# Latent attention: one key projection for two heads, another order of rotary product and taps, and a LayerNorm sum placed elsewhere

## The reference, cut to what matters

```python
def conformer_conv(conv_in, conv_w, conv_b, ln_g, ln_b, w_conv_out):
    a, gt = jnp.split(conv_in, 2, axis=-1)
    z = a * jax.nn.sigmoid(gt)
    z = lax.conv_general_dilated(...)          # 31 taps, one filter per channel, 512 channels
    z = layer_norm(z + conv_b, ln_g, ln_b)
    return jax.nn.silu(z) @ w_conv_out

def mla_attention(c_q, c_kv, k_rope_raw, cos, sin, ...):   # 8 heads
    q = rms_norm_2(c_q, q_norm_g) @ w_uq       # 384 -> 8 * (64 + 32)
    kv = rms_norm_2(c_kv, kv_norm_g) @ w_ukv   # 256 -> 8 * (64 + 64)
    q_rope, k_rope = apply_rope(...), apply_rope(k_rope_raw, cos, sin)
    ... # per head: softmax of q_nope @ k_nope + q_rope @ k_rope, causal, times v
    return o @ w_mla_out
```

## Time and profile before

| | |
|---|---|
| median of 3 runs | 2503.52 us (2503.4 to 2503.57) |
| profiled execution | 2503.53 us, of it span 2501.7 us |
| PE busy | 2487.2 us (99%) |
| DVE busy | 1991.2 us (80%) |
| ACT busy | 1244.3 us (50%) |
| POOL busy | 305.2 us (12%) |
| steps 0 to 17 of the latent attention | 1811.5 to 1979.2 us of the span |

### The profile page before, as it was taken

The page is one execution under the profiler, slowest core; times in us unless marked ns, Lnnn a source line. Parts: engine busy times, 40 slices in busy tenths (PEclk is TensorE's granted clock), DMA queues, the critical chain, the costliest instruction groups (busy, mean ns, idle before and its releaser), DMA issues.

```text
span 2501.7 us, 36450 instructions
## 1 busy us (share of the span) xinstructions
PE 2487.2 (99%) x14212; PEld 2186.6 (87%) x14212; DVE 1991.2 (80%) x2830; ACT 1244.3 (50%) x1975; POOL 305.2 (12%) x250
## 2 busy tenths in 40 slices
PE   9999999999999999999999999999999999999998
PEld 7999988889999889999888899998888888888887
DVE  7878867778888688887777888876899786788873
ACT  6444444444444454444554544445577535654552
POOL 4000001320000000000023100000187221200002
PEclk9999999999999999999999999999999999999999
DMA  5333332223333323334323233334333333233331
GB/s 158 99 96 99 101 104 84 80 87 100 99 102 108 112 85 99 102 98 122 101 60 93 80 104 97 112 103 136 86 74 78 126 93 110 84 108 105 102 100 59
DMA packets 487297, 246.83 MB, mean 99 GB/s; under 512 B 42321, under 2 KB 483926, under 8 KB 486870
## 3 DMA queue, kind: packets, MB, share of 16 engines
q1 hardware_dynamic: 486674, 244.19, 33.9%
q10 hardware_dynamic: 452, 0.32, 0.0%
HBM read 240.27 MB, written 4.19 MB: 98 GB/s over the span
## 4 chain that ended last, share of the span: by engine, by line
PE 95%; DVE 2%; ACT 1%; issue 0%; DMA 0%; POOL 0%; DVEq 0%
PE bank L893 8%; PE bank L892 8%; PE bank L891 8%; PE bank L774 6%; PE bank L776 6%; PE bank L775 6%; PE psS L913 4%; PE psS L914 4%; PE psS L915 4%; PE bank L1452 3%; PE psT L957 2%; PE psT L958 2%; PE psT L959 2%; PE psT L774 2%; PE psT L776 2%; PE psT L775 2%
## 5 line engine op out<-in xcount | busy, mean ns | idle before, releaser
L2267 DVE TENSOR_TENSOR wlo<-raw,whi 128x1024 fp32r<-128x1024 f32 (+2 forms) x212 | 289.0, 1365 | 49.2 <-ACT whi L1582 45.9
L774 PE MATMUL bank<-xhl,whi 128*128 128x512 f32 x672 | 264.7, 394 | 0.0
L775 PE MATMUL bank<-xhl,whi 128*128 128x512 f32 x672 | 262.1, 390 | 0.0
L776 PE MATMUL bank<-xhl,wlo 128*128 128x512 f32 x672 | 262.0, 390 | 0.0
L891 PE MATMUL bank<-xshl,whi 128*128 128x256 f32 x840 | 238.0, 283 | 0.0
L893 PE MATMUL bank<-xshl,wlo 128*128 128x256 f32 x840 | 238.0, 283 | 0.0
L892 PE MATMUL bank<-xshl,whi 128*128 128x256 f32 x840 | 237.9, 283 | 0.0
L1582 ACT ACTIVATE whi<-raw 128x1024 fp32r<-128x1024 f32 (+2 forms) x209 | 214.5, 1030 | 37.3 <-PE bank L776 20.4
L2330 DVE TENSOR_TENSOR wlo<-tw,whi 128x1024 fp32r<-128x1024 f32 x140 | 171.6, 1226 | 61.5 <-ACT whi L1622 61.3
L913 PE MATMUL psS<-hhi,whi 128*128 128x512 f32 x488 | 191.8, 393 | 0.0
L914 PE MATMUL psS<-hlo,whi 128*128 128x512 f32 x488 | 191.7, 393 | 0.0
(11 more groups left out here) (703 smaller groups left out, 7099.7 us busy)
## 6 DMA issues: line engine op xcount, KB each, us to landing
raw<-in_ffn_wg SPq DMA_DIRECT2D x88, 512.0 KB
raw<-in_ffn_wu SPq DMA_DIRECT2D x88, 512.0 KB
raw<-in_w_in SPq DMA_DIRECT2D x53, 512.0 KB
raw<-in_w_mlp SPq DMA_DIRECT2D x40, 512.0 KB
raw<-in_ffn_wd SPq DMA_DIRECT2D x48, 256.0 KB
raw<-in_ffn_wd SPq DMA_DIRECT2D x24, 448.0 KB
raw<-in_ffn_wd SPq DMA_DIRECT2D x48, 192.0 KB
raw<-in_ffn_wd SPq DMA_DIRECT2D x48, 128.0 KB
```

The costliest lines, as they stand in the source:

```text
L774: pe.matmul(dest, a, rhs_hi(k), start=start and k == 0, stop=False)
L775: pe.matmul(dest, a, rhs_lo(k), start=False, stop=False)
L776: mm = pe.matmul(dest, b_, rhs_hi(k), start=False, stop=stop and k == tiles - 1)
L2267: dve.tensor_tensor(wlo[:, a:a + n], raw[:, a:a + n], whi[:, a:a + n].bitcast(F32), ALU.subtract).then_inc(s_split, 1)
```

## The change

- Keys: `w_ukv`'s key columns of heads h and h+1 (h even) are loaded together, 128 columns, and projected at once; head h's key comes out in rows 0 to 63 of the bank, head h+1's in rows 64 to 127. Odd heads have no key projection. Their query comes out with the rotary rows first (32 columns and their swapped halves in rows 0 to 63) and the rest in rows 64 to 127, so that it meets its key; the rotary table and the key's rotary rows exist in both places (one more ACT copy).
- The odd head's key stays in `bank[1]` until the step after its partner's projection (steps 3, 7, 11), where ACT and DVE take it out behind the exponentials and the reciprocal; before step 0 for head 1.
- Head units are split only as far as they are filled: 640 columns for even heads, 384 for odd ones, where it was 1024.
- Queues: in steps 4, 8 and 12 DVE makes the rotary product (heads 3, 5, 7) ahead of the taps; in step 8 the eviction, too, is ahead of the taps; in step 0 the split comes after the rotary product. ACT copies the query's other rows ahead of the head's weight split.
- LayerNorm: the two additions of squares stand at the end of DVE's step 13, where they stood in step 14 behind the row maxima; the variance comes behind the reciprocal of step 14; on PE the sum of squares goes in ahead of tile 7 of step 14's unit, where it was tile 5.
- Several semaphores get a second user later in the program and a new name for it (not shown in the diff below).

```diff
+        HEAD_PARTS = [("q", 0), ("k", 0), ("k", 1), ("q", 1)]
+        for h in range(2, H2, 2):
+            HEAD_PARTS += [("q", h), ("k", h), ("k", h + 1), ("q", h + 1)]
+        HEAD_TILES = {C_IN + ORDER.index(("head", h)): QC if h % 2 else QC + KVC for h in range(H2)}
...
+        def head_rows(h):
+            return (slice(NOPE, P), slice(0, NOPE)) if h % 2 else (slice(0, NOPE), slice(NOPE, P))
+
+        ROPE_FIRST = range(4, 2 * H2 - 2, 4)
...
-                    for a, col, n in ((0, i * QK, QK), (QK, r0 + HALF, HALF), (QK + HALF, r0, HALF)):
+                    if i % 2:
+                        parts = ((0, r0, ROPE), (ROPE, r0 + HALF, HALF), (ROPE + HALF, r0, HALF), (NOPE, i * QK, NOPE))
+                    else:
+                        parts = ((0, i * QK, QK), (QK, r0 + HALF, HALF), (QK + HALF, r0, HALF))
+                    for a, col, n in parts:
                         sp.dma_start(dq[:, :, a:a + n], c2(wq, 0, QC, col, n)).then_inc(landed[slot(c)], 16)
-                    sp.dma_start(dk, c2(t["w_ukv_2"], 0, KVC, i * P)).then_inc(landed[slot(c)], 16)
+                    for k in range(0 if i % 2 else KVC):
+                        sp.dma_start(dk[:, k].rearrange("p (h n) -> p h n", h=2), vw[:, k, i:i + 2, 0, :]
+                                     ).then_inc(s_kw if k else landed[slot(c)], 16)
...
-                    elif s // 2 < H2:
-                        pe.wait_ge(h_lo, 2 * (s // 2) + 2)
+                    elif s // 2 < H2 and s // 2 % 2 == 0:
+                        pe.wait_ge(h_lo, head_part("k", s // 2 + 1))
...
-                in_unit(*FILL[s], ready=(lambda k: conv_square_sums() if k == 5 else None) if s == LN_VAR + 1 else None)
+                in_unit(*FILL[s], ready=(lambda k: conv_square_sums() if k == 7 else None) if s == LN_VAR + 1 else None)
...
-                if s % 2 == 0 and h < H2:
+                if s % 2 == 0 and h < H2 and h % 2 == 0:
                     pe.wait_ge(s_i2, evicted(*FILL[s]))
                     project(h, "k")
...
-                a, n = slot(c) * UNIT, tiles * P
+                a, n = slot(c) * UNIT, HEAD_TILES.get(q + c, tiles) * P
...
+            act.activation(rope[0:NOPE, :], rope[NOPE:P, :], ACT.Copy).then_inc(s_rs, 1)
...
+                if s % 4 == 3 and (s + 3) // 2 < H2:
+                    head_k((s + 3) // 2)
...
-                if s == LN_VAR + 1:
-                    for j in (0, 2):
-                        dve.wait_ge(s_lsq, j + 2)
-                        dve.tensor_tensor(ln_sq[j][:, :], ln_sq[j][:, :], ln_sq[j + 1][:, :], ALU.add).then_inc(s_tap, 1)
-                    variance(LNVAR, tap_b, CW, SUMLN)
...
                 if s == LN_VAR + 1:
+                    variance(LNVAR, tap_b, CW, SUMLN)
                     newton(LNVAR, acc)
...
-                if s in (4, 6):
+                if s in (4, 6, 8):
                     evict(*FILL[s])
+                if s in ROPE_FIRST:
+                    head_rope(h)
+                if s % 4 == 3 and (s + 3) // 2 < H2:
+                    head_k((s + 3) // 2)
                 if s:
                     taps(DVE_SHARE.get(("slot", s), 0))
...
-                    if s != 2:
+                    if s > 2 and s not in ROPE_FIRST:
                         head_rope(h)
...
+                if s == LN_VAR:
+                    for j in (0, 2):
+                        dve.wait_ge(s_lsq, j + 2)
+                        dve.tensor_tensor(ln_sq[j][:, :], ln_sq[j][:, :], ln_sq[j + 1][:, :], ALU.add).then_inc(s_tap, 1)
-                if s % 2 == 0 and h < H2:
+                if s % 2 == 0 and h < H2 and h % 2 == 0:
                     head_k(h)
```

More of the change, by code:

```diff
@@ L1130, in project @@
                     mm = pe.matmul(dest, wl, chunk(lath, l0 + k), start=False, stop=k == n - 1)
-                mm.then_inc(h_q if part == "q" else s_used, 1)
+                mm.then_inc(h_q if part == "q" and h % 2 == 0 else s_used, 1)
             def mla_scores(s):
@@ L1907, in glu_tanh, with head_copy, head_scaled @@
                 act.activation(g, g, ACT.Tanh, scale=0.5).then_inc(s_th, 1)
-            def head_q(h):
-                bb = h % 2 * S
-                act.wait_ge(h_q, h + 1)
+            def head_copy(h):
+                rows = head_rows(h)[0]
+                if h % 2:
+                    act.wait_ge(s_used, unit_of("head", h) + 1)
+                else:
+                    act.wait_ge(h_q, h // 2 + 1)
                 if h == 1:
                     act.wait_ge(s_z, 3)
-                act.activation(tmp[0][0:NOPE, :], bank_of[("hq", h)][0:NOPE, :], ACT.Copy).then_inc(h_cp, 1)
+                act.activation(tmp[0][rows, :], bank_of[("hq", h)][rows, :], ACT.Copy).then_inc(h_cp, 1)
+            def head_scaled(h):
+                bb = h % 2 * S
                 act.wait_ge(h_rp, h + 1)
@@ L1919, in head_k @@
             def head_k(h):
-                bb = h % 2 * S
-                act.wait_ge(s_used, unit_of("head", h) + 1)
-                act.activation(k2h[0:NOPE, bb:bb + S], bank_of[("hk", h)][0:NOPE, :], ACT.Copy).then_inc(h_hi, 1)
+                bb, rows = h % 2 * S, head_rows(h)[0]
+                act.wait_ge(s_used, unit_of("head", h - h % 2) + 1)
+                if h >= 2:
+                    act.wait_ge(a_sc, ATT1 + 2 * h - 2)
+                act.activation(k2h[rows, bb:bb + S], bank_of[("hk", h - h % 2)][rows, :], ACT.Copy).then_inc(h_hi, 1)
             split(unit_of("q", 2) + AHEAD, 0)
@@ L1973, in _ @@
                 some = min(share, 1)
+                left = share
                 split(unit_of(*FILL[s]) + AHEAD, 0)
-                if s:
+                if s > 1:
                     products(some)
+                    left -= some
                 if s < MLA_STEPS:
@@ L2023, in _ @@
                     act.activation(pt2h[:, :], psT[:, 0:(TB + 1) * P], ACT.Copy).then_inc(a_th, 1)
-                products(share - (3 * some if s else 1))
-                if s % 2 == 0 and h < H2:
+                products(left)
+                if s % 2 == 0 and h < H2 and h % 2 == 0:
                     head_k(h)
@@ L2059, in cross_qhi @@
             def cross_qhi(h):
-                act.wait_ge(s_x2, h + 1)
-                act.activation(chunk(q3h, h), tmp[h % 2][:, :], ACT.Copy).then_inc(s_x2h, 1)
+                act.wait_ge(s_qs, 5 * L + h + 1)
+                act.activation(chunk(q3h, h), tmp[h % 2][:, :], ACT.Copy).then_inc(s_qh, 1)
             def cross_khi(h):
@@ L2726, in head_rope @@
             def head_rope(h):
-                dve.wait_ge(h_q, h + 1)
+                rows = head_rows(h)[1]
+                if h % 2:
+                    dve.wait_ge(s_used, unit_of("head", h) + 1)
+                else:
+                    dve.wait_ge(h_q, h // 2 + 1)
                 if h == 1:
                     dve.wait_ge(s_z, 3)
-                dve.tensor_tensor(tmp[0][NOPE:P, :], bank_of[("hq", h)][NOPE:P, :], rope[NOPE:P, :], ALU.mult).then_inc(h_rp, 1)
+                    dve.wait_ge(s_rs, 4)
+                dve.tensor_tensor(tmp[0][rows, :], bank_of[("hq", h)][rows, :], rope[rows, :], ALU.mult).then_inc(h_rp, 1)
             def head_q(h):
                 bb = h % 2 * S
-                dve.wait_ge(h_hi, 2 * h + 1)
+                dve.wait_ge(h_hi, head_part("q", h))
                 dve.scalar_tensor_tensor(q2l[:, bb:bb + S], tmp[0][:, :], QK ** -0.5,
@@ L2791, in _ @@
             for j in range(2):
-                for n, r in enumerate((NOPE, QK)):
+                for n, r in enumerate(KEY_ROPE_AT[j]):
                     dve.wait_ge(s_krh, 2 * j + n + 1)
@@ L2855, in _ @@
                     glu(2)
+                    head_rope(h)
+                    split(unit_of(*FILL[s]) + AHEAD, 0)
                 if s == 2:
@@ L2868, in _ @@
                     dve.tensor_tensor(tmp[2][:, :], chunk(zc, 0), chunk(zc, 2), ALU.add).then_inc(s_tap, 1)
-                if s not in (0, 2, 4, 6):
+                if s not in (0, 2, 4, 6, 8):
                     evict(*FILL[s])
```

103 lines of the change are left out of this document (55 added, 48 removed).

## The result

The changed kernel takes 2512.01 us (median of 6 runs, 2510.46 to 2512.58) against 2503.44 (6 runs, 2503.30 to 2503.57): a ratio of 1.0033, 95% interval 1.0023 to 1.0043. It is 8.6 us slower; the prediction said 2505.6, in a range up to 2508.8. The profiled execution took 2511.57 us, 8.0 more than the one of before. One execution of run a_two, further down, ran at a mean granted clock of 0.65 and took 3505.64 us; it was the one that was profiled, and it is left out of that run's figures.

A forecast was written before the change was run, and what follows sets the result against it. PE was taken to bound the kernel, with DVE nearly as full in the attention steps. The terms -5.4 + 4.3 + 1.1 + 0.3 + 1.2 + 1.2 - 0.35 - 0.25 = +2.1 on 2503.5 gave 2505.6 us, range 2501.8 to 2508.8.

The forecast's parts named there:

- POOL's hold on DVE: Steps 4 and 8: the moved split and query low part fall beside POOL's tap additions; +1.2 us, bound 3.8.
- rival (c): Step 12: the 4.3 us standstill makes PE's clock fall; 6 us at half speed cost 3.0, giving 2508.6; chance 0.13.
- Key projections, -5.4: Steps 0, 4, 8 and 12: six matmuls each go, 1.36 us a step, -5.4 us on PE.
- Step 12, +4.3: LayerNorm's sum: PE waits for DVE's chunk addition, since head 7's rotary product stands ahead of the taps; +4.3 us.
- the eight transposes: Sign for rival (c): after the start's standstill, transposes took 0.25 us each against 0.14 in step 8, suggesting a slow restart.
- Scores of steps 10 and 6: PE waits there because DVE's work in steps 8 and 4 grows behind the early rotary product; +1.1 and +0.3 us.
- key projection of step 10: DVE comes late to step 10, so PE waits for the eviction that this projection needs; +1.2 us.
- LayerNorm, -0.35: Step 14: the sum of squares, two tiles later, should find its additions ready, removing PE's 0.35 us wait.
- Scores of step 4, -0.25: The 0.27 us wait before these scores should go, since DVE's split of step 2 has fewer columns; -0.25 us.
- At nothing: Shorter splits of steps 6 and 10, low parts moved into steps 3, 7, 11, ACT's table copy, extra DMA issues: no cost.
- (d): Steps 4 and 8: POOL's full bound of 3.8 us instead of 1.2, giving 2508.2; chance 0.07.

The follow-up runs named there:

- a_two: Changed kernel with two taps instead of four between head 7's rotary product and the chunk addition in step 12: 2509.07 us.
- b_k1: Kernel before the change with the key projections of odd heads cut to one matmul of six, nothing else changed: 2503.21 us.
- a_rope12_poolcut: a_rope12 with POOL's additions of taps cut to 32 of 512 columns, the rest left out: 2499.40 us.
- a_rope12: Changed kernel with head 7's rotary product put back behind the taps of step 12; heads 3 and 5 stay ahead: 2505.42 us.
- a_rope12_ln: a_rope12 with the LayerNorm part undone too: additions of squares at the head of step 14, their sum behind the sixth tile: 2508.68 us.
- a_poolcut: Changed kernel with POOL's additions of taps cut to 32 of 512 columns, the rest left out: 2504.79 us.
- a_rope0: Changed kernel with all rotary products of odd heads behind the taps, as before the change: 2504.68 us.
- a_three: Changed kernel with three taps instead of four between head 7's rotary product and the chunk addition in step 12: 2511.77 us.
- v3: Changed kernel with taps moved into DVE's idle time, step 10's eviction ahead of taps, and ACT's key copy ahead of the tap products: 2503.94 us.

## Why the prediction was wrong, point by point

Two steps of the prediction failed. It put POOL's hold on DVE at +1.2 us, with a bound of 3.8, and cutting POOL's additions gives back 6.0. And its sum put the fall of the clock, which it had as rival (c), at nothing, where the trace shows 2.5. That is 4.8 and 2.5 of the 6.4 us between forecast and measurement; the other terms come to -0.9 together. The change is slower, where no difference was forecast.

- **Key projections, -5.4.** PE does lose these matmuls: from the query projection of step 0 to the next scores it is 1820.49 - 1818.45 = 2.04 us, where before 1.36 more came. The size of the term is right, but the removal does not pay "directly". b_k1 keeps 0.3 of 4.5, so alone it is worth nothing that can be told; only with POOL out of the way (a_rope12_poolcut) are 4.1 of the 5.4 kept. The prediction read that DVE was as full as PE, and drew from it some chains, but not that the whole stretch had no room: from the scores of step 1 to those of step 12 DVE stands idle for 2.4 of 104.5 us in the trace of before.
- **Step 12, +4.3.** Right: 3.99 of waiting, 4.2 from where PE could have started, at the instruction and for the reason that were named. a_rope12 shows it; 0.3 of waiting would be there without the swap.
- **Clock, rival (c).** Given 0.13, and it came: 2.5 us by the trace, and by the medians 6.6 less 3.7, 2.9. No row gave the 6 us at half speed that its price was worked out from; it was 5.2. That the gaps of the trace of before were too short to show a fall was true, but it was no reason against one. Its sign for a slow restart, the eight transposes, doesn't hold either: the granted clock reads 1.00 there too (6.00 to 8.00). The Trainium skill (TensorE: Matmul & The Clock Gate, section "Part 1: The HAM clock gate"), which the prediction named, says that the clock falls back after idling. In this case the trace agrees, the clock being 0.50 behind the standstill and 1.00 before it.
- **Scores of steps 10 and 6, +1.1 and +0.3; key projection of step 10, +1.2.** The three waits are there and are 1.2, 1.2 and 1.7 us (1907.40 to 1909.05 less 0.48, 1867.14 to 1868.79 less 0.48, 1918.83 to 1920.97 less 0.46). Without POOL's additions 0.75 at the scores of step 10 and 0.83 at the key projection remain, and this view shows none at the scores of step 6: what the chains alone give, 1.6.
- **POOL, +1.2, bound 3.8.** The term that was mis-sized most: 6.0. The bound took the two instructions which the change moves, in each of steps 4 and 8. In these four the trace of the changed kernel has 3.3 us of stretch (a split of 1.96, low parts of 1.78 and 1.78), so as a bound for them it was good. But 7.4 of the 10.7 lie in other instructions, and most splits of steps 1 to 11 were already stretched in the trace of before (1440 ns in the median, 1215 without POOL). There it cost 0.3; the longer steps of PE covered it, and part of that cover is what the change removes.
- **LayerNorm, -0.35.** The wait is gone, as said, but its worth is larger: in the new order the old place would wait 2.02 (a_rope12_ln). The 0.35 in the trace of before showed that DVE's chain ends there, and not what that place costs once PE comes to it sooner.
- **Scores of step 4, -0.25.** It failed: 0.31 us of waiting there and 0.26 in step 2, since DVE's splits in steps 1 and 2 are no shorter in time.
- **At nothing.** The low part of the probabilities in steps 5 and 9 (1.9) and the unit of step 7 (0.6) were not. Both are gone in a_poolcut, so they are part of POOL's 6.0.
- **Rivals as if they excluded each other.** (c) and (d) came together. From the runs: 6.6 (the order of step 12) + 6.0 (POOL) - 4.1 (what a_rope12_poolcut is under before) = +8.5, and 8.6 was measured. These are differences along one chain of kernels, so that they add up says little; what checks the terms is the last: -5.4 + 1.6 (the chains without POOL) - 0.35 = -4.15, against -4.1. The range ended at 2508.8 because each rival was added to the forecast alone; with the prices of (c) and (d) together it would have ended near 2511.2.

What stays open: why the clock falls in some executions and not in others behind the same waits, and how much of the spread of 2 us between runs of the changed kernel that is; and how POOL's 6.0 divide between the larger stretch, the lost cover and ACT's waits for POOL.

## What to carry to other kernels

Where two engines are full in the same stretch, work taken from one of them may be worth nothing until the other gets shorter too; test it first by leaving the work out in the old kernel, which here would have shown 0.3 us for 4.5. Look for instructions whose longest duration is far above their shortest in the old trace: such a stretch may be free today (0.3 us here) and cost when its cover is removed (6.0). And don't put an instruction that waits for a late result of the bound engine ahead of ready work on which that engine waits next: here one such swap cost 3.7 us of waiting and 2.5 of clock.

## What the runs showed of the hardware that was not expected

- A fall of the granted clock from 1.00 to 0.50 after a standstill of 2.75 us (a_rope0, step 5), and in a_three and a_rope12_ln after two waits of 1.22 and 0.92 us with less than a microsecond of work between them; the same two waits left the clock at 1.00 in the traces of the changed kernel and of a_rope12, and so did single standstills of 1.92 us (b_k1) and 2.02 us (a_rope12_ln). The kernel before, whose longest wait in these steps is 0.35 us, spreads over 0.6 us between runs, the changed one over 2.1.
- One standstill, two prices: behind 3.99 us the clock was down before PE started again in the changed kernel (2.5 us lost), and in a_poolcut it fell only after PE had started (0.89 from 1938 to 1940, 0.50 in the two microseconds after; the sum starts at 1938.34). There the swap cost 5.4 us in all, against 6.6.
- GpSimd's additions stretch VectorE's two-input instructions by up to 1.1 us each. In v3, where idle time was taken from VectorE's queue, the median split went from 1.44 to 1.77 us; the time won was largely lost again to the stretch.
